# First normalisation of a two-block transformer kernel: tokens turned unscaled, scales applied to the outputs

## The chip, the cores and the metric

The kernel runs on one core of a Trainium2 chip. The metric is the device time of one execution in microseconds. A core has five engines with queues of their own: TensorE (PE; its weight loads are shown as PEld), VectorE (DVE), ScalarE (ACT), GpSimd (POOL) and SyncE (SP), which here issues the loads. They wait for each other through semaphores, which the kernel writes out by hand.

## What is computed

Two transformer blocks on 256 tokens of width 1024, all in float32. Only the opening of the first block is touched by the change:

```python
def rmsnorm(x, g):
    y = x * lax.rsqrt(jnp.mean(x * x, axis=-1, keepdims=True) + EPS)
    return y * g

hn = rmsnorm(h, attn_norm_g)
q, k, v, u, vg = jnp.split(hn @ w_in, [512, 1024, 1536, 2048], axis=-1)
sb_out = stick_breaking_attention(q, k, v)        # 8 heads of 64
sg_out = chunked_spatial_gating(u, vg, ...)       # u = gelu(u); vg = rmsnorm(gelu(vg))
h = h + concat(rmsnorm(sb_out), rmsnorm(sg_out)) @ w_out
```

Behind it come a mixture of 32 experts in 4 groups (top 1 group, top 2 experts), then a second block with differential attention, sparse attention, a cross-attention over a memory, and a layer that gathers rows of a large table (`in_uv`) for each token.

Since the norm multiplies each token (row of x) by one number s, and the gain multiplies each feature, (s x g) @ W = s ((x g) @ W): the number s can be applied before the product or to its outputs.

## The kernel before

**Operands.** Products with the input weights run in a rounded 32-bit type in three terms: a value is split into a high part (rounded) and a low part (what is left), and high*high, high*low and low*high are summed. For weights, ScalarE makes the high part (`high_quarters`, L192, 1024 columns at a time) and VectorE the low part (`low_quarters`, L199), each quarter of a 128x4096 piece. Pieces are `in0` (queries), `in1` (keys), `in4` (gate values, called g), `in3` (u), `in2` (v), `out0` and `out1`. There are two buffers for high parts, so `in4` waits until the query products are done with `in0`, and `in3` until the key products are done with `in1`.

**Tokens.** x (256 tokens, two tiles of 128) has to stand with its features on the partitions. `turn_pe` (L213) turns 16 blocks of 128x128 by TensorE into four PSUM banks, `turn_act` (L286) multiplies each of the eight chunks by the gain and rounds it (high part, XH), `turn_dve` (L293) makes its low part (XL).

**Order of the opening.** It is written by hand, an ordered list of steps for each engine (`a_pe`, `a_act`, `a_dve`), each of which raises the engine's semaphore by one. `mixers_sp` issues x, the identity, the small vectors, the first quarter of `in0`, its other three quarters, `in1`, `in4` and so on; `load_piece` waits until the piece two before has landed. When x is there, ScalarE (L300) and VectorE (L303) sum the squares of one token tile each, VectorE makes the mean (L297), GpSimd raises it to the power -1/2 (`rstd_pool`, L314), and ScalarE (L464) and VectorE (L306) each write one scaled tile into XZ. TensorE fills the time with products of no use (`spare`, 256 columns), turns XZ, and goes on, quarter by quarter as the parts arrive:

```python
turn_pe(pe, XZ, a_pe, "turn")
spare(pe, 6, 6)
turned_pair(pe, "in0", X2, a_dve, a_dve, "x", a_pe, 4)   # q0, q1
for m in (2, 3): turned(pe, "in0", ...)                  # q2, q3
for m in range(4):                                       # k0..k3, banks 2, 3, 2, 3
    if m >= 2: pe.wait_ge(*a_act.at(f"k{m - 2}"))
    turned(pe, "in1", ...)
```

The queries and keys come out turned (128 features x 256 tokens). ScalarE copies them from PSUM into `aq` (L472, times 0.125) and `ak` (L476). Then TensorE makes the scores (z0 to z2) and the units g (`in4`) and u (`in3`), in which the tokens are on the partitions. ScalarE rounds `in3`, takes Abs, Exp and Ln of the scores (L480, L485, L490), then GELU of g (L493), of u (L501), and later copies v. The u products wait for the GELU of g, since they write to the same banks.

**Behind it.** The units of the first block, the output projection, routing, and from about 130 us the experts, whose weights stream through eight slots; a slot's load is issued when TensorE has done with what it held (L185). The second block starts at about 583 us, and from 864 us on rows of `in_uv` are gathered by GpSimd (L2549) and multiplied (L2326).

## Time and profile before

| what | us |
|---|---|
| median of 3 runs | 1532.43 |
| lowest and highest | 1529.96, 1535.26 |
| profiled execution | 1534.07 |
| its span | 1532.0 |
| TensorE busy in it | 1252.2 (82%) |
| VectorE, ScalarE, GpSimd busy | 740.6, 469.5, 273.9 |
| bytes moved | 544.10 MB, mean 355 GB/s |

The span is the time from the first to the last instruction of the profiled execution; its own time lies 2.1 us above the span. In the rows below, L and a number is a line of the kernel, an arrow `<-` in an operation goes from what it reads to what it writes (out<-in), and `xN` counts instructions that were merged into one row. Matmuls overlap in the pipeline, so a duration of one is longer than the distance between two starts.

### The profile page before, as it was taken

How to read it: one execution, taken by the hardware profiler on the slowest of the kernel's cores; microseconds unless marked ns; L12 is line 12 of the kernel's file. 1: busy time of each engine (PE TensorE's matmuls, PEld its weight loads, DVE VectorE, ACT ScalarE, POOL GpSimd, SP SyncE). 2: the span in 40 equal slices, each digit the busy share in tenths (PEclk: the TensorE clock that was granted, in tenths of full speed). 3: DMA queues.
4: the chain of work that ended last, by engine and by line, in shares of the span. 5: the costliest groups of instructions: out<-in, count | busy, mean ns of one | idle time of the engine just before them, and what ended most of it. 6: DMA issues, size and time to landing. Idle time of an engine off the chain costs nothing.

```text
span 1532.0 us, 21054 instructions
## 1 busy us (share of the span) xinstructions
PE 1252.2 (82%) x8433; PEld 733.8 (48%) x8433; DVE 740.6 (48%) x1771; ACT 469.5 (31%) x1251; POOL 273.9 (18%) x287
## 2 busy tenths in 40 slices
PE   7999999999999987999999886888755645555465
PEld 7787565665555546977755453355311111111112
DVE  5544222212211115457722686676666676667454
ACT  5833011010100006456632244243323232323223
POOL 0000000000000001001000233434533333333331
PEclk9999999999999998999999999899977778777868
DMA  9548999999999998543471399999999999999996
GB/s 391 197 164 343 428 424 426 424 425 427 423 427 424 425 411 329 196 167 124 157 309 55 145 422 420 421 375 420 421 421 421 421 421 421 421 422 420 422 422 276
DMA packets 64583, 544.10 MB, mean 355 GB/s; under 512 B 6624, under 2 KB 7136, under 8 KB 12640
## 3 DMA queue, kind: packets, MB, share of 16 engines
q1 hardware_dynamic: 26160, 273.84, 43.6%
q0 software_dynamic: 38016, 268.45, 42.3%
q8 instruction: 69, 1.13, 0.3%
q10 hardware_dynamic: 304, 0.39, 0.1%
q14 instruction: 34, 0.28, 0.1%
HBM read 541.61 MB, written 1.05 MB: 354 GB/s over the span
## 4 chain that ended last, share of the span: by engine, by line
DMA 45%; PE 39%; DVE 5%; issue 4%; ACT 4%; POOL 2%; DVEq 0%; POOLq 0%; SPq 0%; ACTq 0%
PE PS L203 37%; DMA AR<-in_uv,CO 28%; DMA AR<-in_w_up 13%; DMA Wk<-in_w_up 2%; DMA EX<-in_w_up 2%; DVE AR L2326 2%; PE PS L213 2%; POOL AR L2549 1%; ACT HI L192 1%; ACT SM L2215 0%; ACT Wk L2221 0%; POOL AR L2525 0%; DMA CO<-in_const 0%; DVE XH L957 0%; ACT RW L2211 0%
## 5 line engine op out<-in xcount | busy, mean ns | idle before, releaser
L203 PE MATMUL PS<-AR,Wk 64*64 64x512 f32 (+4 forms) x2096 | 389.1, 716 | 186.3 <-ACT Wk L2221 179.6
L2326 DVE CUSTOM_DVE_ANT_0 AR<-AR,PS 128x1024 f32<-128x1024 f32 x192 | 233.9, 1221 | 171.2 <-DMA AR<-in_uv,CO 169.8
L203 PEld LDWEIGHTS PS<-AR,Wk 64*64 64x64 f32 (+3 forms) x2096 | 109.9, 157 | 417.8 <-ACT Wk L2221 282.5
L2549 POOL DMA_INDIRECT AR<-in_uv,CO x186 | 178.4, 959 | 295.1 <-PE PS L203 256.3
L203 PE MATMUL PS<-AR 128*64 128x256 f32 (+3 forms) x1656 | 192.3, 382 | 9.3 <-DMA AR<-in_w_up 8.7
L203 PEld LDWEIGHTS PS<-AR 128*64 128x64 f32 (+3 forms) x1656 | 119.7, 138 | 88.0 <-issue 19.3
L314 POOL TENSOR_TENSOR ST<-ST 128x2 f32<-128x2 f32 (+3 forms) x14 | 12.8, 915 | 779.4 <-DVE ST L1121 473.1
L2211 ACT ACTIVATE RW<-SM 128x2 f32<-128x2 f32 (+1 forms) x132 | 27.0, 205 | 395.3 <-DVE SM L2326 395.2
L199 DVE TENSOR_TENSOR LO<-AR,HI 128x1024 fp32r<-128x1024 f32 x76 | 89.5, 1225 | 54.6 <-ACT HI L192 54.6
L999 DVE TENSOR_TENSOR AR<-AR,PS 128x256 f32<-128x256 f32 x32 | 13.5, 422 | 195.1 <-ACT AR L856 195.1
L203 PE MATMUL PS<-Wk,AR 128*128 128x128 f32 (+2 forms) x816 | 97.5, 313 | 2.0 <-DMA Wk<-in_w_up 1.2
L203 PEld LDWEIGHTS PS<-Wk,AR 128*128 128x128 f32 (+1 forms) x816 | 83.7, 177 | 27.8 <-issue 12.5
L203 PE MATMUL PS<-XN,Wk 64*64 64x512 f32 (+1 forms) x368 | 66.3, 726 | 19.1 <-ACT Wk L2221 18.8
L1007 DVE SCALAR_TENSOR_TENSOR YL<-PS,Wk,YH 128x512 fp32r<-128x512 f32 x32 | 24.0, 751 | 112.3 <-ACT YH L860 112.3
L856 ACT ACTIVATE AR<-PS 128x256 f32<-128x256 f32 x32 | 12.3, 384 | 214.0 <-PE PS L203 214.0
L2221 ACT ACTIVATE Wk<-Wk,SM 128x64 f32<-128x64 f32 x256 | 75.5, 340 | 4.3
L192 ACT ACTIVATE HI<-AR 128x1024 fp32r<-128x1024 f32 x76 | 75.6, 1055 | 1.2 <-DMA AR<-in_w_in 1.2
L203 PE MATMUL PS<-HI,XH 128*128 128x512 f32 (+1 forms) x176 | 69.8, 397 | 4.2 <-ACT AR L1510 2.5
L203 PE MATMUL PS<-EX,Wk 64*64 64x512 f32 (+1 forms) x240 | 46.1, 781 | 26.2 <-ACT Wk L2221 26.2
L203 PE MATMUL PS<-HI,XL 128*128 128x512 f32 (+1 forms) x176 | 67.4, 383 | 0.0
L203 PE MATMUL PS<-LO,XH 128*128 128x512 f32 (+1 forms) x176 | 67.3, 382 | 0.0
L2215 ACT ACTIVATE SM<-RW 128x1 f32<-128x1 f32 x256 | 61.9, 287 | 12.8 <-ACT RW L2211 0.7
(308 smaller groups left out, 1803.8 us busy)
## 6 DMA issues: line engine op xcount, KB each, us to landing
AR<-in_w_up SPq DMA_DIRECT2D x24, 2048.0 KB, 14.7
AR<-in_w_down SPq DMA_DIRECT2D x24, 2048.0 KB, 14.7
AR<-in_w_gate SPq DMA_DIRECT2D x24, 2048.0 KB, 14.7
AR<-in_w_in SPq DMA_DIRECT2D x14, 2048.0 KB, 9.7
EX<-in_w_gate SPq DMA_DIRECT2D x4, 2048.0 KB, 15.3
Wk<-in_w_up SPq DMA_DIRECT2D x4, 2048.0 KB, 14.7
EX<-in_w_down SPq DMA_DIRECT2D x4, 2048.0 KB, 14.7
Wk<-in_w_gate SPq DMA_DIRECT2D x4, 2048.0 KB, 14.7
```

The source lines that it names most:

```text
L192: act.activation(hi[:, cs], w[:, cs], ACT.Copy).then_inc(*steps.up(f"{name}.{k}"))
L199: eng.tensor_tensor(lo[:, cs], w[:, cs], hi[:, cs].bitcast(F32), ALU.subtract).then_inc(*steps.up(f"{name}.{k}"))
L203: return pe.matmul(o, l, r, start=start, stop=stop, skip_group_check=True)
L213: return pe.transpose(o, i, ident[0:n, 0:n])
L314: pool.tensor_tensor(ST[:, a:b], ST[:, a:b], HALF[:, 0:b - a], ALU.pow).then_inc(*rms.up(site))
L999: dve.tensor_tensor(HM[:, b, :], SG[:, b, :], P(4 + b)[:, 256:512], ALU.mult).then_inc(*m_dve.up(f"h{ex}"))
L1007: dve.scalar_tensor_tensor(YL[:, b, :], P(6), SLOT_GATE[:, b:b + 1], YH[:, b, :].bitcast(F32), ALU.mult, ALU.subtract).then_inc(*m_dve.up( ...
L2211: act.activation(GEL[:, e:e + g1 - g0], DT[:, g0:g1], ACT.Gelu).then_inc(*a_own.up())
L2215: t = act.activation(DT[:, g:g + 1], BGf[:, g:g + 1], ACT.Copy, scale=GEL[:, e + g - g0:e + g - g0 + 1])
L2221: act.activation(DG[:, g % 8, :], ID64, ACT.Copy, scale=DT[:, g:g + 1]).then_inc(diags, 1)
L2326: t = dve.tensor_tensor_reduce(r, r, P(6 if g < 128 else 2, 2), 1.0, 0.0, ALU.mult, ALU.add, DT[:, g:g + 1])
L2549: pool.indirect_dma_start(RING[k], None, uv, bass.IndirectOffsetOnAxis(ap=IDX[:, g:g + 1], axis=0)).then_inc(g_in[k], 16)
```

## The change

- TensorE turns x itself (`H`) as soon as it and the identity have landed. XZ is no longer written with scaled tokens.
- ScalarE and VectorE begin with the turned chunks x0 and x1, then take the first quarter of `in0`, then the other chunks. The squares are summed behind the quarters of `in0`.
- GpSimd's power and the mean stay as they are, later. Of the two resulting columns VectorE makes two diagonal matrices; TensorE multiplies them by a matrix of ones, behind the queries (step `wide`), so that each partition holds the scales of all 256 tokens; VectorE copies this to `WIDE_X`.
- VectorE, no longer ScalarE, takes queries and keys out of PSUM, multiplied by `WIDE_X`, interleaved with the low parts of `in4`.
- For g, u and v, which have tokens on the partitions, ScalarE applies the scale as the operand of its GELU or copy.
- The first 16 spare products of 256 columns become 32 of 128 columns with zeros, which wait for the zeros alone.

Step lists (`a_pe`, `a_act`, `a_dve`) follow; they are left out of the diff.

```diff
@@ -348,6 +348,9 @@
         T1 = w2(3072)
         VG = w2(1024, "p (t n) -> p t n", t=2)
         blocks = [(0, 0), (0, 1), (1, 1)]
+        WIDE_X = MX[:, 0, 0:256]
+        DIAG_X = MX[:, 1, 0:256].rearrange("p (t n) -> p t n", t=2)
+        ONES_X = MX[:, 0, 256:384]
 
         def mixers_sp(sp):
             sp.dma_start(H, x.rearrange("(t p) d -> p t d", p=128)).then_inc(ld_x, 16)
@@ -373,22 +376,25 @@
 
         def mixers_pe(pe):
             pe.wait_ge(wm_set, 1)
-            spare(pe, 6, 8)
-            pe.wait_ge(*a_dve.at("mean"))
-            spare(pe, 6, 8)
+            for _ in range(32):
+                mm(pe, P(6)[:, 0:128], WMt[:, 128:256], WMt[:, 128:256], True, True)
             pe.wait_ge(ld_id, 16)
-            pe.wait_ge(*a_act.at("xs0"))
-            pe.wait_ge(*a_dve.at("xs1"))
-            turn_pe(pe, XZ, a_pe, "turn")
+            pe.wait_ge(ld_x, 16)
+            turn_pe(pe, H, a_pe, "turn")
+            pe.wait_ge(wm_set, 2)
             spare(pe, 6, 6)
             turned_pair(pe, "in0", X2, a_dve, a_dve, "x", a_pe, 4)
             for m in (2, 3):
                 turned(pe, "in0", X2, P(m % 2)[:, 0:256], m).then_inc(*a_pe.up(f"q{m}"))
+            for tt in range(2):
+                pe.wait_ge(*a_dve.at(f"diag{tt}"))
+                t = mm(pe, P(6)[:, tt * 128:tt * 128 + 128], ONES_X, DIAG_X[:, tt, :], True, True)
+            t.then_inc(*a_pe.up("wide"))
             for m in range(4):
                 if m >= 2:
-                    pe.wait_ge(*a_act.at(f"k{m - 2}"))
+                    pe.wait_ge(*a_dve.at(f"k{m - 2}"))
                 turned(pe, "in1", X2, P(2 + m % 2)[:, 0:256], m, *((a_dve,) if m == 0 else ())).then_inc(*a_pe.up(f"k{m}"))
-            pe.wait_ge(*a_act.at("k3"))
+            pe.wait_ge(*a_dve.at("k3"))
             for b, (kt, qt) in enumerate(blocks):
                 for h in range(8):
                     r = slice(64 * (h % 2), 64 * (h % 2) + 64)
@@ -402,6 +408,7 @@
                         pe.wait_ge(*a_act.at(f"{before}{tt}"))
                     tokens(pe, name, X2, P(6 + tt), tt, *((a_dve,) if tt == 0 else ())).then_inc(*a_pe.up(f"{tag}{tt}"))
 
+            pe.wait_ge(*a_dve.at("wide"))
             unit("in4", "g", None)
             unit("in3", "u", "g")
             pe.wait_ge(ld_co, 16)
@@ -458,22 +465,17 @@
                     out_part_pe(pe, j, tt, range(4)).then_inc(*a_pe.up(f"r{j}{tt}"))
 
         def mixers_act(act):
+            act.wait_ge(ld_sm, 16)
+            turn_act(act, X2, sm["g_attn"], a_act, "x", a_pe, "turn", range(2))
+            high_quarters(act, "in0", a_act, range(1), (ld_in0, 16))
+            turn_act(act, X2, sm["g_attn"], a_act, "x", a_pe, "turn", range(2, 8))
+            high_quarters(act, "in0", a_act, range(1, 4))
             act.wait_ge(ld_x, 16)
-            square_sum(act, H[:, 0, :], XS[:, 0, :], ST[:, 0:1]).then_inc(*a_act.up("sq"))
-            act.wait_ge(*rms.at("x"))
-            act.activation(XZ[:, 0, :], H[:, 0, :], ACT.Copy, scale=ST[:, 0:1]).then_inc(*a_act.up("xs0"))
-            act.wait_ge(ld_sm, 16)
-            high_quarters(act, "in0", a_act, range(1), (ld_in0, 16))
-            turn_act(act, X2, sm["g_attn"], a_act, "x", a_pe, "turn")
-            high_quarters(act, "in0", a_act, range(1, 4))
+            square_sum(act, H[:, 0, :], XZ[:, 0, :], ST[:, 0:1]).then_inc(*a_act.up("sq"))
             high_quarters(act, "in1", a_act)
-            for m in range(4):
-                act.wait_ge(*a_pe.at(f"q{m}"))
-                act.activation(aq[:, m, :], P((4, 5, 0, 1)[m])[:, 0:256], ACT.Copy, scale=0.125).then_inc(*a_act.up(f"q{m}"))
+            act.wait_ge(*a_pe.at("q3"))
             high_quarters(act, "in4", a_act)
-            for m in range(4):
-                act.wait_ge(*a_pe.at(f"k{m}"))
-                act.activation(ak[:, m, :], P(2 + m % 2)[:, 0:256], ACT.Copy, scale=1.0).then_inc(*a_act.up(f"k{m}"))
+            act.wait_ge(*a_pe.at("k3"))
             high_quarters(act, "in3", a_act)
             for b in range(3):
                 act.wait_ge(*a_pe.at(f"z{b}"))
@@ -488,9 +490,10 @@
             for b in range(3):
                 l = T1[:, b * 1024:(b + 1) * 1024]
                 act.activation(l, l, ACT.Ln, bias=1.0).then_inc(*a_act.up(f"ln{b}"))
+            act.wait_ge(*rms.at("x"))
             for tt in range(2):
                 act.wait_ge(*a_pe.at(f"g{tt}"))
-                act.activation(VG[:, tt, :], P(6 + tt), ACT.Gelu_apprx_tanh).then_inc(*a_act.up(f"g{tt}"))
+                act.activation(VG[:, tt, :], P(6 + tt), ACT.Gelu_apprx_tanh, scale=ST[:, tt:tt + 1]).then_inc(*a_act.up(f"g{tt}"))
             act.wait_ge(*a_act.at("g1"))
             for tt in range(2):
                 t = square_sum(act, VG[:, tt, :], MX[:, tt, 512:1024], ST[:, 4 + tt:5 + tt])
@@ -498,7 +501,7 @@
             high_quarters(act, "in2", a_act)
             for tt in range(2):
                 act.wait_ge(*a_pe.at(f"u{tt}"))
-                act.activation(U1[:, tt, :], P(6 + tt), ACT.Gelu_apprx_tanh).then_inc(*a_act.up(f"u{tt}"))
+                act.activation(U1[:, tt, :], P(6 + tt), ACT.Gelu_apprx_tanh, scale=ST[:, tt:tt + 1]).then_inc(*a_act.up(f"u{tt}"))
             high_quarters(act, "out0", a_act)
             for b in range(3):
                 l = T1[:, b * 1024:(b + 1) * 1024]
@@ -514,7 +517,7 @@
             t.then_inc(*a_act.up("sqg"))
             for tt in range(2):
                 act.wait_ge(*a_pe.at(f"v{tt}"))
-                act.activation(AV[:, tt, :], P(6 + tt), ACT.Copy).then_inc(*a_act.up(f"v{tt}"))
+                act.activation(AV[:, tt, :], P(6 + tt), ACT.Copy, scale=ST[:, tt:tt + 1]).then_inc(*a_act.up(f"v{tt}"))
             turn_act(act, X2, sm["g_mix"], a_act, "m", a_pe, "turn2", range(4, 8))
             high_quarters(act, "out1", a_act)
             act.wait_ge(*a_pe.at("pv"))
@@ -527,22 +530,40 @@
             zeros = AR[:, 6 * 4096:6 * 4096 + 128]
             dve.memset(zeros, 0.0).then_inc(*own.up())
             dve.wait_ge(*own.at())
-            dve.tensor_copy(WMt[:, 128:256], zeros)
+            dve.tensor_copy(WMt[:, 128:256], zeros).then_inc(wm_set, 1)
             dve.wait_ge(ld_id, 16)
             dve.tensor_copy(WMt[:, 0:128], ident).then_inc(wm_set, 1)
+            dve.wait_ge(ld_sm, 16)
+            turn_dve(dve, X2, sm["g_attn"], a_act, a_dve, "x", range(2))
+            low_quarters(dve, "in0", a_act, a_dve, range(1))
+            turn_dve(dve, X2, sm["g_attn"], a_act, a_dve, "x", range(2, 8))
+            low_quarters(dve, "in0", a_act, a_dve, range(1, 4))
+            dve.memset(ONES_X, 1.0).then_inc(*a_dve.up("ones"))
             dve.wait_ge(ld_x, 16)
-            square_sum_dve(dve, H[:, 1, :], XS[:, 1, :], ST[:, 1:2]).then_inc(*a_dve.up("ss"))
+            square_sum_dve(dve, H[:, 1, :], XZ[:, 1, :], ST[:, 1:2]).then_inc(*a_dve.up("ss"))
             dve.wait_ge(*a_act.at("sq"))
             dve.wait_ge(*a_dve.at("ss"))
             mean(dve, ST[:, 0:2], D).then_inc(*a_dve.up("mean"))
             dve.wait_ge(*rms.at("x"))
-            scaled(dve, XZ[:, 1, :], H[:, 1, :], ST[:, 1:2]).then_inc(*a_dve.up("xs1"))
-            dve.wait_ge(ld_sm, 16)
-            low_quarters(dve, "in0", a_act, a_dve, range(1))
-            turn_dve(dve, X2, sm["g_attn"], a_act, a_dve, "x")
-            low_quarters(dve, "in0", a_act, a_dve, range(1, 4))
-            for name in ("in1", "in4", "in3"):
-                low_quarters(dve, name, a_act, a_dve)
+            for tt in range(2):
+                scaled(dve, DIAG_X[:, tt, :], ident, ST[:, tt:tt + 1]).then_inc(*a_dve.up(f"diag{tt}"))
+            low_quarters(dve, "in1", a_act, a_dve)
+            dve.wait_ge(*a_pe.at("wide"))
+            dve.tensor_copy(WIDE_X, P(6)[:, 0:256]).then_inc(*a_dve.up("wide"))
+            dve.wait_ge(*a_dve.at("wide"))
+
+            def evac(dst, tag, banks, ms, scale=1.0):
+                for m in ms:
+                    dve.wait_ge(*a_pe.at(f"{tag}{m}"))
+                    dve.scalar_tensor_tensor(dst[:, m, :], P(banks[m])[:, 0:256], scale, WIDE_X, ALU.mult, ALU.mult).then_inc(
+                        *a_dve.up(f"{tag}{m}"))
+
+            evac(aq, "q", (4, 5, 0, 1), range(4), 0.125)
+            low_quarters(dve, "in4", a_act, a_dve, range(2))
+            evac(ak, "k", (2, 3, 2, 3), (0,))
+            low_quarters(dve, "in4", a_act, a_dve, range(2, 4))
+            evac(ak, "k", (2, 3, 2, 3), (1, 2, 3))
+            low_quarters(dve, "in3", a_act, a_dve)
             dve.wait_ge(ld_co, 16)
             for b, (kt, qt) in enumerate(blocks):
                 s = SPL[:, b * 1024:(b + 1) * 1024]
```

## Rows read from the trace of the kernel before

**Rows 1.** The page, chain that ended last: shares of the span by engine
```profile
DMA 45%; PE 39%; DVE 5%; issue 4%; ACT 4%; POOL 2%; DVEq 0%; POOLq 0%; SPq 0%; ACTq 0%
```

**Rows 2.** Chain of waits in order of time: start us, us, what
```profile
1.25 4.60 DMA CO<-in_const
...
7.61 0.71 POOL ST L314
...
16.11 21.86 PE PS L203 x180
...
38.00 0.38 ACT Wk L476
...
54.12 30.72 PE PS L203 x128
...
317.63 14.69 DMA AR<-in_w_up
...
1114.70 34.62 DMA AR<-in_uv,CO
```

**Rows 3.** DMA issues of the first 60 us: count, KB each, us to landing
```profile
AR<-in_w_in SPq DMA_DIRECT2D x1, 1536.0 KB, 10.3
```

**Rows 4.** Timeline of the first 17 us: start us, us, engine, work, [idle before <-releaser]
```profile
1.02 0.23 DVE L530 CAST WM<-AR 128x128 fp32r<-128x128 f32 x1
...
2.69 0.45 SPq L357 DMA_DIRECT2D AR<-in_w_in  x1
...
6.15 3.78 PE L203 MATMUL PS<-WM 128*128 128x256 f32 x16 [6.15 <-DVE WM L532]
...
9.40 1.04 ACT L192 ACTIVATE HI<-AR 128x1024 fp32r<-128x1024 f32 x1
...
9.73 2.65 PE L213 MATMUL PS<-CO,AR 128*128 128x128 f32 x16
10.54 1.23 DVE L199 TENSOR_TENSOR LO<-AR,HI 128x1024 fp32r<-128x1024 f32 x1 [1.44 <-ACT HI L192]
10.82 3.03 ACT L286 ACTIVATE XH<-PS,SM 128x256 fp32r<-128x256 f32 x8 [0.38 <-PE PS L213]
11.70 3.23 DVE L293 SCALAR_TENSOR_TENSOR XL<-PS,SM,XH 128x256 fp32r<-128x256 f32 x8
...
13.69 3.00 ACT L192 ACTIVATE HI<-AR 128x1024 fp32r<-128x1024 f32 x3
...
14.84 3.49 DVE L199 TENSOR_TENSOR LO<-AR,HI 128x1024 fp32r<-128x1024 f32 x3
...
16.11 0.39 PE L203 MATMUL PS<-XH,HI 128*128 128x256 f32 x1 [1.58 <-DVE LO L199]
```

**Rows 5.** Timeline of the first expert, TensorE's loads of weights
```profile
138.86 0.31 PEld L203 LDWEIGHTS PS<-WM,PG 128*128 128x128 f32 x2
...
139.09 0.19 PEld L203 LDWEIGHTS PS<-PG,XGH 128*128 128x128 f32 x1
```

**Rows 6.** TensorE by line and form: count, busy us, mean ns, idle before
```profile
L203 PE MATMUL PS<-Wk,AR 128*128 128x128 f32 x512 | 62.8, 283 | 0.8 <-ACT Wk L1840 0.8
```

**Rows 7.** Timeline of ScalarE, and of VectorE in the first expert
```profile
17.86 3.91 ACT L192 ACTIVATE HI<-AR 128x1024 fp32r<-128x1024 f32 x4 [1.17 <-DMA AR<-in_w_in]
...
38.28 3.89 ACT L192 ACTIVATE HI<-AR 128x1024 fp32r<-128x1024 f32 x4
...
53.48 1.09 ACT L493 ACTIVATE AR<-PS 128x512 f32<-128x512 f32 x2
...
138.16 0.42 DVE L999 TENSOR_TENSOR AR<-AR,PS 128x256 f32<-128x256 f32 x1 [5.09 <-ACT AR L856]
```

**Rows 8.** Waits by engine and line, 0 to 60 us: total, times, longest
```profile
PE PS L203 <- ACT AR L493: 1.6, 1, 1.6
```

**Rows 9.** Stretches: busy us of PE, PEld, DVE, ACT, POOL; PEclk, DMA share, GB/s
```profile
584.00:596.00 12.00, 5.44 (x24) 5.20 (x25) 9.32 (x15) 9.37 (x16) 1.01 (x1) 0.53 0.97 407
596.00:620.00 24.00, 23.71 (x189) 23.50 (x188) 13.05 (x20) 12.91 (x21) 5.68 (x2) 0.95 0.55 216
```

More of the change, by code:

```diff
@@ L325, in program @@
         gated, broken = [f"m{c}" for c in range(4, 8)], fours("m")
-        a_pe = Steps(sem("a_pe"), [*split_steps("turn"), *fours("q"), *fours("k"), "z0", "z1", "z2", *twos("g"), *twos("u"),
+        a_pe = Steps(sem("a_pe"), [*split_steps("turn"), *fours("q"), "wide", *fours("k"), "z0", "z1", "z2", *twos("g"), *twos("u"),
                                    "sum0", "sum1", "sum2", "space", *twos("v"), "turn2.2", "turn2.3", "pv", "turn2.0", "turn2.1",
                                    "r00", "r01", "r10", "r11"])
-        a_act = Steps(sem("a_act"), ["sq", "xs0", "in0.0", *eights("x"), "in0.1", "in0.2", "in0.3", *split_steps("in1"), *fours("q"),
-                                     *split_steps("in4"), *fours("k"), *split_steps("in3"), "abs", "exp", "ln0", "ln1", "ln2",
+        a_act = Steps(sem("a_act"), ["x0", "x1", "in0.0", *eights("x")[2:], "in0.1", "in0.2", "in0.3", "sq", *split_steps("in1"),
+                                     *split_steps("in4"), *split_steps("in3"), "abs", "exp", "ln0", "ln1", "ln2",
                                      *twos("g"), "sqv", *split_steps("in2"), *twos("u"), *split_steps("out0"), "e0", "e1", "e2", "sqg",
                                      *twos("v"), *gated, *split_steps("out1"), "sqb", *broken])
-        a_dve = Steps(sem("a_dve"), ["ss", "mean", "xs1", "in0.0", *eights("x"), "in0.1", "in0.2", "in0.3", *split_steps("in1"),
-                                     *split_steps("in4"),
+        a_dve = Steps(sem("a_dve"), ["x0", "x1", "in0.0", *eights("x")[2:], "in0.1", "in0.2", "in0.3", "ones", "ss", "mean", "diag0", "diag1",
+                                     *split_steps("in1"), "wide", *fours("q"), "in4.0", "in4.1", "k0", "in4.2", "in4.3", "k1", "k2", "k3",
                                      *split_steps("in3"), "sp0", "sp0m", "sp1", "sp2", "sp2m", "meanv", "vg", *split_steps("in2"),
```

## The prediction

> **What bounds the kernel now.** I read the page first, then the chain of waits over the first 130 us, then the timeline of each engine over the first 60 us, and last what bounds the rest. The shares of the chain [rows 1] say what the whole is made of: DMA 45% and PE 39%. The change touches the first 54 us of 1532 directly, so the question is what is late there, and whether a microsecond won there reaches the end.
>
> The chain [rows 2] shows three links of the opening: POOL's power of the norm at 7.61, then PE's unbroken 21.86 us of query and key products (180 of them, 0.121 us each) from 16.11, then ScalarE from 38.00 until PE takes over at 54.12. From there PE leads until the expert weights do (317.63, a wait of 14.69 us for a piece of w_up), and at the end the gathered rows (34.62 us in one wait). Everything behind 54 us is started by steps of PE or by what they release; what comes earlier there should come earlier at the end, less whatever a transfer takes back.
>
> The opening in detail: x and identity have landed by 5.85 [rows 2]. Then squares, mean, power and two scaled copies run before PE may turn anything: the turns start at 9.73 [rows 4]. But the turned tokens are only one of two things that PE wants. The other is in0. Its last three quarters are issued at 2.69 [rows 4] and land 10.3 later [rows 3], at 12.99. ScalarE rounds them from 13.69, VectorE subtracts from 14.84, and PE, idle for 1.58, goes on at 16.11 [rows 4]. So of the whole norm chain only the 0.70 between 12.99 and 13.69 is not covered by the load of in0. That is what I expect to be worth having, and it is the point at which I part from the obvious count (the turns could start 3.8 earlier).
>
> **Part by part.**
>
> Norm out of the way. Removed ahead of the turns: squares, mean, power, two scaled copies. ScalarE now has x0 and x1, then the first quarter of in0 (landed by 9.40, where it starts now [rows 4]), then x2 to x7. The first quarter ends at 10.4; six turned chunks at 3.03/8 = 0.38 [rows 4] bring it to 12.7. The next quarter then waits for the landing at 12.99 instead of starting at 13.69. VectorE follows ScalarE by 10.54 - 9.40 = 1.14 in this pattern. Its first low quarter runs 10.54 to 11.77, six chunks at 3.23/8 = 0.40 end at 14.2, and the second quarter of in0 can be subtracted from 12.99 + 1.14 = 14.13. Two limits that nearly coincide; PE resumes at 15.41 instead of 16.11. **Gain 0.70.**
>
> Warm-up products. 16 of 256 columns behind the identity become 32 of 128 columns from 1.27, as soon as the zeros are written [rows 4]. Before, 16 took 3.58 (6.15 to 9.73 [rows 4]), 0.22 each. Products with 128 columns of this rounded type stand in the expert stage only: two of them, whose loads take 0.31 for two with 0.19 for one, come 0.12 apart at the full clock [rows 5]. They are as slow as those with twice the columns. So the bounds are 0.11 each at the low clock (half of 0.22) and 0.25 (twice 0.12). I take 0.22, as the 0.12 row is the nearest in kind: until the clock rises 24 or so, then the rest at 0.12, together some 6, ending at 7.3. The first turns then wait 1.5 behind them, yet x0 and x1 are ready by 8.7, before the first quarter of in0 has landed. **Cost nothing**, because the load hides it; without that cover it would be 1.5. The Trainium skill (TensorE: Matmul & The Clock Gate, Wait — 56ns, not 53.3ns?) gives 107 ns for 128 columns cold and 56 ns warm; by it the 32 would be over at 4.7, before x has landed, and the row (0.12 warm) speaks against it for this type.
>
> Spreading the scales. Two products of ones with a diagonal, 128x128 in plain f32, go between queries and keys on PE's queue, where nothing hides them. Such products cost between 62.8/512 = 0.12 [rows 6] and their full 0.28 with 0.2 for the change of type. Bounds for the pair 0.25 to 0.77; I take 0.5. They wait for the diagonals, ready at 20.4 (VectorE: in0's lows to 17.6, ones and squares 1.4, mean 0.2, POOL 0.71 [rows 2] and handing over, two small scalings), well before queries end at 25.6. **Cost 0.5.**
>
> Copies of queries and keys move from ScalarE to VectorE. A pass over 128x256 from PSUM with a second operand is 0.42 [rows 7] against 0.38. VectorE's queue: in1's lows end at 25.0 (20.4 and four at 1.16); it waits there for the wide products at 26.1; the copy and four query passes end at 28.2; two quarters of in4 at 30.5; k0 at 31.0. PE needs the bank of k0 for k2 at 26.1 + 5.8 = 31.9. k1 is copied at 33.7 and wanted at 34.8. **Cost nothing**, slack 0.9 and 1.1. Queued behind VectorE's wait for the wide products is everything up to in3's lows; PE itself waits for it only at k2, k3 and the scores.
>
> ScalarE no longer copies k3 before it rounds in3. That copy starts at 38.00 [rows 2] and in3's quarters at 38.28 [rows 7], behind it. Now they start as PE ends the keys. From there to the first GELU at 53.48 ScalarE never waits [rows 7], and PE sat idle 1.6 waiting for it [rows 8]. So this 0.28 is on the path, and the scores, 0.04 later behind VectorE's pass, are covered by in3's four quarters (3.89). **Gain 0.28.**
>
> Scales on GELU and on v: a per-partition operand in place of a constant. ScalarE's turned chunk with such an operand is 0.38, the k3 copy without one 0.38. Nothing. ScalarE's squares now fall between in0 and the landing of in1 (it waits until 17.86 anyway [rows 7]). No DMA is added or moved; SP's waits for queries and keys fall 0.2 to 0.7 earlier.
>
> Sum: -0.70 + 0.5 - 0.28 = **-0.5 us**. The profiled execution took 1534.07 (span 1532.0), so it would be 1533.6; it lies 1.6 above the median of the runs, 1532.43, and against that median the forecast is **1531.9**. About 0.3% (4.6 us) is what a measurement can tell from no change; the three runs alone lie 5.3 apart. So: no measurable change.
>
> **Rivals.**
>
> PE's clock falls in the opening. Until now PE pauses once, for 1.58 [rows 4]. After the change it has done its warm-up and turns by about 10, waits for the first low quarter until 11.8, works 1.4, waits until 15.4. Later in this kernel 12 us with PE busy for 5.4 had a granted clock of 0.53, and the 24 behind it, full work, 0.95 [rows 9]. At the low one of the two levels, 1.2 GHz, a product costs 0.22 instead of 0.121, and PE's run is on the path. 24 us at 0.95 is 2.4 at the low level, 1.2 lost: net +0.7. If it stayed low for all of the 84 queries left and more, the loss is 0.1 a product: 50 products cost 5, and from there on the kernel is slower measurably; all 84 cost 8.4, net +7.9, 1540.3. For it: the opening has less PE work per microsecond than before. From 7.3 to 15.4 it has about 4 us of work in 8, hardly more than those 5.4 in 12. Against: here the pauses are of 1.8 and 2.2, and it comes to them at the full clock from unbroken work. The Trainium skill (TensorE: Matmul & The Clock Gate, HAM oscillation — how this bites in real kernels) warns of just this, that waits for loads between bursts put the array back to half rate; by that rule the gain is gone.
>
> Warm-up too long. At 0.25 each the 32 end at 9.3; turns, x0 and x1 come at 11.0, in0's first quarter at 12.0, VectorE's chunks at 15.7, PE resumes at 17.0: 0.9 late, net +1.1, 1533.5.
>
> VectorE becomes the bound. If its six passes before k2 took 0.84 each, k2 would stall by 1.6, net +1.1. Against: 0.42 in the trace and slack 0.9.
>
> The full norm chain was what mattered. Then PE resumes up to 3.8 earlier, net -3.6, 1528.8. Against it is the landing of in0 at 12.99; even so it would not be measurable.
>
> **How the numbers follow.** Forecast (a gain of up to 1 us) 0.50, clock falls briefly 0.27, clock stays low 0.04, warm-up too long 0.10, VectorE 0.05, full chain 0.04. Only one of them is beyond 4.6 us. The rest of both tails is the scatter of 5.3 between equal runs. Faster 0.05, same 0.89, slower 0.06. Range: from the full chain's 1528.8 less a little scatter, 1528.0, to the warm-up's 1533.5 with 2.5 of scatter and a little more for a clock low for 20 or 30 products, 1536.5.
>
> **What would show it.** PE's first turn near 7.3 (4.7: products at 0.11; 9.3: at 0.25). in0's second quarter rounded at 13.0 behind a landing, not behind ScalarE's own work. PE back at 15.4. Two wide products costing about 0.5 between queries and keys. in3's quarters at 37.8 on ScalarE, GELU at 53.0, PE's u products at 53.6 (54.12 before). Granted clock 1.00 from 12 to 54. Wrong if PE resumes before 15 (the landing is not the bound), if query products run at 0.2 apart, or if the 0.5 is not seen at the first expert.

## The result and the profile after

The changed kernel takes 1536.63 us (median of 20 runs) against 1532.47 for the kernel before (20 runs): a ratio of 1.0027, interval 1.002 to 1.0034. It is 4.1 us slower. The forecast was 1531.9, no measurable change, with a range up to 1536.5. One of the 20 runs of the changed kernel took 2582 us and is not in the ratio.

| landmark in the profiled execution | before | after | later by |
|---|---|---|---|
| PE resumes with the second quarter of in0 | 16.11 [rows 2] | 17.24 | 1.13 |
| in3's quarters on ScalarE, behind the keys | 38.28 [rows 7] | 41.06 | 2.78 |
| PE starts the u products | 54.12 [rows 2] | 57.01 | 2.89 |
| execution (span) | 1534.07 (1532.0) | 1539.85 (1537.8) | 5.8 |

This execution lies 3.2 above the median of its kernel. The page of it:

```profile
span 1537.8 us, 21101 instructions
...
PE 1267.4 (82%) x8453; PEld 742.3 (48%) x8453; DVE 742.9 (48%) x1782; ACT 466.4 (30%) x1242; POOL 274.8 (18%) x287
...
PE 47%; DMA 37%; issue 5%; ACT 4%; DVE 4%; POOL 1%; DVEq 0%; POOLq 0%; ACTq 0%; SPq 0%
```

DMA's share of the chain was 45% and is 37%, PE's 39% and is 47%. That is no effect of the change: a second profile of the same changed kernel has 43% and 41%, and one with ScalarE's table load moved ("Table load early" below) 52% and 30%. ScalarE's opening (start us, us, engine, line, work, [idle before]):

```profile
9.36 1.28 ACT L286 ACT_TABLE_LOAD   x1 [9.36 <-PE PS L213]
10.66 0.84 ACT L286 ACTIVATE XH<-PS,SM 128x256 fp32r<-128x256 f32 x2
11.38 1.06 ACT L192 ACTIVATE HI<-AR 128x1024 fp32r<-128x1024 f32 x1
12.33 2.29 ACT L286 ACTIVATE XH<-PS,SM 128x256 fp32r<-128x256 f32 x6
14.47 3.00 ACT L192 ACTIVATE HI<-AR 128x1024 fp32r<-128x1024 f32 x3
```

The first row was not in the count: a load of ScalarE's function table, 1.28 us, now begins only when the first turns are done. TensorE's side of the same stretch:

```profile
1.31 7.09 PE L203 MATMUL PS<-WM 128*128 128x128 f32 x32 [1.31 <-DVE WM L533]
8.20 3.46 PE L213 MATMUL PS<-CO,Hs 128*128 128x128 f32 x16
11.41 0.96 PE L203 MATMUL PS<-WM 128*128 128x256 f32 x6
...
17.24 0.39 PE L203 MATMUL PS<-XH,HI 128*128 128x256 f32 x1 [1.79 <-DVE LO L199]
```

The 32 warm-up products last 7.09 (0.22 each, to the last), so the turns (the 16 blocks of x that TensorE turns) start at 8.20 and not at 5.9, and all 16 of them run at the low pace as well, 0.21 each, where eight turns later in this kernel take 0.87. The granted clock of the profile reads 1.00 in this stretch all the same, as it does in the opening of the kernel before; that TensorE is at the lower of its two levels here is read from the pace alone. The chain of waits, start us, us, what:

```profile
17.24 23.80 PE PS L203 x184
...
41.06 3.90 ACT HI L192 x4
...
57.01 30.74 PE PS L203 x128
...
133.57 6.45 PE PS L203 x57
```

From 17.24 to the end of the keys PE takes 23.80 instead of 21.86 [rows 2]. Two stretches of it (busy us of PE, PEld, DVE, ACT, POOL; then PEclk, DMA share, GB/s):

```profile
16.00:20.00 4.00, 2.76 (x16) 2.77 (x17) 4.00 (x6) 4.00 (x6) 0.00 (x0) 0.77 0.99 426
20.00:26.00 6.00, 6.00 (x46) 6.00 (x45) 5.07 (x9) 2.29 (x3) 0.75 (x2) 0.87 1.02 426
```

The granted clock was 0.77 and 0.87 there, so 0.23 x 4 + 0.13 x 6 = 1.7 us of full clock were lost by these figures; it was 1.00 in the kernel before. A profile without the fall, below, puts the loss at 1.49.

### The profile page after: what moved, and what is told of

The parts are those of the page before. It is cut to its first block, busy times and chain, and to the rows that moved or that the text cites. A ratio compares the mean times of both kernels' runs of the same rounds, so it can differ in the third digit from the quotient of the medians.

```text
span 1537.8 us, 21101 instructions
## 1 busy us (share of the span) xinstructions
PE 1267.4 (82%) x8453; PEld 742.3 (48%) x8453; DVE 742.9 (48%) x1782; ACT 466.4 (30%) x1242; POOL 274.8 (18%) x287
## 3 DMA queue, kind: packets, MB, share of 16 engines
q8 instruction: 69, 1.13, 0.3%
HBM read 541.61 MB, written 1.05 MB: 353 GB/s over the span
## 4 chain that ended last, share of the span: by engine, by line
PE 47%; DMA 37%; issue 5%; ACT 4%; DVE 4%; POOL 1%; DVEq 0%; POOLq 0%; ACTq 0%; SPq 0%
PE PS L203 46%; DMA AR<-in_uv,CO 25%; DMA AR<-in_w_up 9%; DMA EX<-in_w_up 2%; PE PS L213 2%; DVE AR L2347 1%; DMA Wk<-in_w_up 1%; ACT HI L192 1%; DMA XN<-in_uv,CO 1%; POOL AR L2570 0%; ACT Wk L2242 0%; ACT SM L2236 0%; POOL AR L2546 0%; ACT Wk L1861 0%; DVE XH L978 0%
## 5 line engine op out<-in xcount | busy, mean ns | idle before, releaser
L203 PE MATMUL PS<-AR,Wk 64*64 64x512 f32 (+4 forms) x2096 | 396.2, 731 | 178.6 <-ACT Wk L2242 161.8
L203 PEld LDWEIGHTS PS<-AR 128*64 128x64 f32 (+3 forms) x1656 | 119.6, 138 | 88.8 <-issue 19.1
L203 PE MATMUL PS<-Wk,AR 128*128 128x128 f32 (+2 forms) x816 | 100.8, 316 | 4.2 <-issue 2.3
L203 PE MATMUL PS<-XN,Wk 64*64 64x512 f32 (+1 forms) x368 | 65.0, 709 | 16.4 <-ACT Wk L2242 15.5
```

The lines of the kernel that those rows point to most:

```text
L203: return pe.matmul(o, l, r, start=start, stop=stop, skip_group_check=True)
```

## The experiments

Each result is a ratio to runs of the kernel before on the same chip. The kernels are told as edits of the changed kernel where nothing else is said.

### Table load early

```diff
+            act.wait_ge(*rms.at("half"))
+            act.activation(ST[:, 62:63], HALF[:, 0:1], ACT.Copy)
             act.wait_ge(ld_sm, 16)
```

> The changed kernel with one tiny ScalarE copy (one column) put ahead of its first waits, so that the 1.28 us load of ScalarE's function table, which in the changed kernel begins at 9.36 behind the first turns, falls into the empty time before x lands. Theory (the table load is on the path of the opening): ScalarE's first turned chunk starts at 9.36 instead of 10.66, the second quarter of in0 is rounded from 13.2 instead of 14.47, PE resumes at 16.0 instead of 17.24, and its u products start 1.2 earlier than 57.01 if the clock falls as before (about 55.8), 2.7 earlier if it doesn't. Total 1.2 to 2.7 below the changed kernel's 1536.6, about 1535. Rival (the landing of in0 at 13.0 and the turns at 8.4 hold it anyway): PE resumes at 17 or later, no difference. Second rival for the clock: it falls again at 18.2 for 3.4 us, as PE's work before it is the same.

Ratio 1.0015 (1.0006 to 1.0024), 1534.95 us. ScalarE's timeline, then the chain:

```profile
0.72 1.28 ACT L469 ACT_TABLE_LOAD   x1 [0.72 <-PEq L2722]
...
9.38 0.84 ACT L286 ACTIVATE XH<-PS,SM 128x256 fp32r<-128x256 f32 x2 [7.16 <-PE PS L213]
...
13.20 3.00 ACT L192 ACTIVATE HI<-AR 128x1024 fp32r<-128x1024 f32 x3
```

```profile
15.96 22.30 PE PS L203 x184
...
54.23 30.73 PE PS L203 x128
```

The load falls into the empty time at 0.72 and everything behind it is 1.28 earlier, as expected. The clock did not fall at all here, so u starts 2.8 earlier, 0.1 behind the kernel before. The opening was put right, and the total was still 2.3 above the kernel before (0.0015 x 1532.9). A pause of 1.25 stands in the turns of the second block, which the next experiments are about.

### Twelve warm-up products

```diff
-            for _ in range(32):
+            for _ in range(12):
```

> The changed kernel with 12 instead of 32 warm-up products, which also brings TensorE's count of instructions back to that of the kernel before. Theory: the 32 products at 0.22 us each (7.09 us) hold up the turns from 5.9 to 8.4, and the table load starts when the first turns are done. With 12 they end at 4.0, turns start at 5.9, the table load at 6.9, x0 at 8.1, first quarter of in0 at 9.4, PE resumes at 15.4, which is 1.8 earlier. If the clock is up by then, u starts 1.8 earlier than 57.01 (55.2), 3.3 earlier if it doesn't fall (53.7). Rival (warm-up is needed for the clock): the granted clock is half for more of the queries than the 3.4 us of the changed kernel, each 3.4 us costing 1.5, and u starts no earlier than 56. On the rest: a pause of 1.29 us in the middle of the turns of the second block (597.87 to 599.16 in the changed kernel, none in the kernel before), which the profile puts down to nothing but issue, is a fetch of TensorE's code; with the old count of instructions it should go, and the second block's first products come 1.0 earlier against the first expert. If it stays, it isn't the count.

Ratio 0.9995 (0.9986 to 1.0004), 1532.75 us: the kernel before's time. ScalarE's timeline:

```profile
7.23 1.28 ACT L286 ACT_TABLE_LOAD   x1 [7.23 <-PE PS L213]
...
12.83 2.95 ACT L192 ACTIVATE HI<-AR 128x1024 fp32r<-128x1024 f32 x3 [0.34 <-DMA AR<-in_w_in]
```

The table load starts at 7.23 and is hidden (the first turns are ready earlier, as they wait for 12 products only), and the second quarter of in0 now starts behind its landing (the idle time is ended by the DMA). This is the bound that the forecast named; PE resumes at 15.20. But the chain shows that this gain of 0.9 was lost again before u:

```profile
15.20 10.80 PE PS L203 x88
...
32.22 6.03 PE PS L203 x48
...
54.22 5.98 PE PS L203 x25
```

Between the 88 products from 15.20 and k2 at 32.22 VectorE is in the chain. Its rows, and GpSimd's:

```profile
27.82 4.01 DVE L199 TENSOR_TENSOR LO<-AR,HI 128x1024 fp32r<-128x1024 f32 x2
31.75 0.41 DVE L558 SCALAR_TENSOR_TENSOR Wk<-PS,Wk 128x256 f32<-128x256 f32 x1
```

```profile
27.20 2.41 POOL L626 TENSOR_TENSOR Wk<-Wk,CO 128x1024 f32<-128x1024 f32 x1 [7.50 <-DMA Wk<-in_w_sp]
```

Two low quarters took 4.01 where they take 2.35 elsewhere, k0 was taken out of PSUM at 31.75 and k2 had waited 0.49 for it. They met GpSimd's multiplication of the spatial weights, which ended at 29.61: the trace has the first of the two at 2.88 (27.82 to 30.70) and the second at 1.21. The second block's turns had no pause.

### Without pauses on TensorE

```diff
+            act.wait_ge(*rms.at("half"))
+            act.activation(ST[:, 62:63], HALF[:, 0:1], ACT.Copy)
...
-            for _ in range(32):
-                mm(pe, P(6)[:, 0:128], WMt[:, 128:256], WMt[:, 128:256], True, True)
+            for _ in range(20):
+                mm(pe, P(6)[:, 0:256].rearrange("p (a n) -> p a n", a=2), WMt[:, 128:256],
+                   bc(WMt[:, 128:256].unsqueeze(1), [128, 2, 128]), True, True)
...
-            spare(pe, 6, 6)
+            spare(pe, 6, 16)
```

and 13 spare products more ahead of the second quarter of in0. The 20 products have 256 columns, all zeros.

> The changed kernel with the early table load, 20 warm-up products of 256 columns of zeros in place of 32 of 128, 16 spare products in place of 6 behind the turns, and 13 more between the first and the second quarter of in0, so that TensorE has hardly a pause. Theory (three things hold it: table load 1.3, late turns, clock 1.5): the turns start at 5.9, PE resumes at 15.4, no fall of the clock at 18, keys end at 37.7, u starts at 53.7 (54.12 before, 57.01 changed). Total 3.3 below the changed kernel by the opening, about 1533, or 1532 if the pause in the second block goes as well: the same as before, not faster. Rival (the first product of the change, unscaled turning, can't reach below the landing of in0): the same 15.4; if PE resumes under 15 the landing is not the bound. Rival on the clock: it falls in spite of the fill, u at 55.2.

Ratio 1.0011 (1.0000 to 1.0023), 1534.49 us. The opening came as expected: PE resumes at 15.01, the landing still the bound, the turns faster (16 in 2.54 instead of 3.46), u at 53.29, which is 0.8 earlier than in the kernel before. The total is nevertheless 1.7 above it. The loss is in the second block, whose spare products before the turns read:

```profile
589.13 1.62 PE L203 MATMUL PS<-WM 128*128 128x256 f32 x6 [6.10 <-issue]
594.34 1.01 PE L203 MATMUL PS<-WM 128*128 128x256 f32 x3 [3.59 <-issue]
```

A pause of 3.59 that the profile puts down to nothing but issue. The label alone says little, since the idle time of about 6 before the nine spare products is called issue in some executions (6.10 here) and VectorE's in others (5.71 in the kernel before). But between the sixth and the seventh spare product the code has no wait. This kernel has 11 more products ahead of the second block than the changed one (8464 against 8453 on the page), and the pause stands 10 products earlier in the program: 3 spare ones and 7 turned blocks. It sits at a place in the code, not at a moment in time.

### The kernel before with 20 more products

```diff
             pe.wait_ge(wm_set, 1)
+            for _ in range(20):
+                mm(pe, P(6)[:, 0:128], WMt[:, 128:256], WMt[:, 128:256], True, True)
+            pe.wait_ge(wm_set, 2)
             spare(pe, 6, 8)
...
-            dve.tensor_copy(WMt[:, 128:256], zeros)
+            dve.tensor_copy(WMt[:, 128:256], zeros).then_inc(wm_set, 1)
```

> The kernel before with 20 products of 128 columns of zeros put ahead of its own warm-up, done before the identity lands, so that nothing in its opening moves, but TensorE's code has the changed kernel's count of instructions. Theory (1.0 of the 4.2 is a fetch of code that has moved into the turns of the second block): opening as before (PE resumes at 16.1, u at 54.1, first expert at 130.6), pause of about 1.3 in the second block's turns, its first products 1.0 later, total 1.0 above the kernel before. Rival (the 1.0 comes from the phase of the clock in the second block, shifted by the late opening, or from scatter): no pause, total the same as before within 0.5.

> The kernel before with 20 early products once more, as the interval of its first runs (0.06% to 0.24%) leaves open whether the shifted code costs 0.9 or 3.7. Theory: 1.0 to 1.5 above the kernel before, pause of about 1.1 in the second block's turns again at the eighth block. Rival (the first result was scatter): within 0.5 of the kernel before.

Ratios 1.0015 (1.0006 to 1.0024) and, on another chip, 1.0010 (1.0000 to 1.0019): 2.3 and 1.5 us, with an opening that is the old one (u at 54.19 and 54.25). Some 1.0 was expected; the intervals, 0.9 to 3.7 and 0.0 to 2.9 us, allow it. The second run's turns in the second block:

```profile
592.48 1.95 PE L213 MATMUL PS<-CO,AR 128*128 128x128 f32 x8 [0.49 <-ACT AR L1464]
595.48 1.97 PE L213 MATMUL PS<-CO,AR 128*128 128x128 f32 x8 [1.05 <-issue]
```

Twenty products that do nothing, in time that was empty, cost 1.5 to 2.3 us 590 us later. The changed kernel has the same pause at the same place (here behind the seventh block, above behind the eighth); the code has no wait between the 16 turns:

```profile
596.13 1.73 PE L213 MATMUL PS<-CO,AR 128*128 128x128 f32 x7 [0.92 <-ACT AR L1482]
599.16 2.08 PE L213 MATMUL PS<-CO,AR 128*128 128x128 f32 x9 [1.29 <-issue]
```

### The changed kernel again

> The changed kernel, unchanged, for a second profile. Open is whether the fall of the granted clock at 18.2 for 3.4 us is part of the change or of that one execution (its 1539.85 lay 3.2 above the median of its runs). Theory: it is of the execution; in this profile the queries may run unbroken, from 17.2 to 27.4, the keys end at 39.5 and u starts at 55.5, 1.4 later than in the kernel before. Rival: the clock falls again, u at 57.0. In both the pause of some 1.3 in the second block's turns is there, as the count of instructions is the same, and the first eight turned blocks stand on the same side of it. Total 1536.6 within 0.7.

Ratio 1.0040 (1.0025 to 1.0056), 1537.84 us, from 6 runs: 6.1 us above the kernel before, where the first measurement gave 4.1 and 1536.6 within 0.7 was expected. The two intervals, 3.8 to 8.6 and 3.1 to 5.2 us, overlap. Its chain:

```profile
17.24 22.31 PE PS L203 x184
...
55.52 30.74 PE PS L203 x128
```

PE resumes at 17.24 again, the clock does not fall, and 184 products take 22.31: u starts 1.40 late instead of 2.89. The fall at 18 is of the execution, not of the kernel. The difference of 22.31 to the 21.86 for 180 [rows 2] is the price of spreading the scales, 0.45 (184 and 180 count instructions; the two products of the step are four). The pause is there again:

```profile
594.99 1.73 PE L213 MATMUL PS<-CO,AR 128*128 128x128 f32 x7 [0.84 <-ACT AR L1482]
597.85 2.08 PE L213 MATMUL PS<-CO,AR 128*128 128x128 f32 x9 [1.13 <-issue]
```

### A long warm-up in few products

```diff
-            for _ in range(32):
-                mm(pe, P(6)[:, 0:128], WMt[:, 128:256], WMt[:, 128:256], True, True)
+            blank(pe, 16)
...
-            spare(pe, 6, 6)
+            spare(pe, 6, 2)
```

Each `blank` product has 512 columns of zeros.

> The changed kernel with its long warm-up kept in time but not in count: 16 products of 512 columns of zeros (about 0.43 each, 6.8 in all) for 32 of 128, and 2 spare products for 6 behind the turns, which brings TensorE's instructions to the count of the kernel before. Table load late, turns late as in the changed kernel. Theory (the late opening and the code fetch are two separate costs): PE resumes at 17.0 to 17.3, u at 55.4 to 57.0, no pause in the second block's turns, total 1.0 to 1.5 below the changed kernel's, about 1535.3. Rival (the count costs nothing by itself; the total follows the opening alone): 1536.6.

Ratio 1.0004 (0.9993 to 1.0015), 1532.48 us. It did not separate what it was made to separate:

```profile
1.31 5.33 PE L203 MATMUL PS<-WM 128*128 128x512 f32 x16 [1.31 <-DVE WM L537]
...
15.29 0.38 PE L203 MATMUL PS<-XH,HI 128*128 128x256 f32 x1 [0.77 <-DVE LO L199]
```

The 16 took 5.33, 0.33 each: eight start 0.43 apart, the rest 0.23, so the clock went up on the way. So they ended at 6.6, and PE resumed at 15.29; the opening was early. The 32 of 128 columns had stayed at 0.22 for 7.09.

### GpSimd's multiplication moved away

```diff
             rstd_pool(pool, a_dve.at("mean"), "x", 0, 2)
+            rstd_pool(pool, a_dve.at("meanv"), "vg", 4, 6)
             pool.wait_ge(ld_ws, 16)
             pool.wait_ge(ld_co, 16)
             pool.tensor_tensor(WS, WS, ...)
-            rstd_pool(pool, a_dve.at("meanv"), "vg", 4, 6)
```

with 12 warm-up products as above.

> The kernel with 12 warm-up products, and GpSimd's multiplication of the spatial weights (2.4 to 3.1 us at 25.95) moved behind its next power of a norm at about 56. In the kernel with 12, PE resumed at 15.2, 0.9 earlier than in the kernel before, yet u started at 54.22, no earlier: VectorE's two low quarters of in4 took 4.01 instead of 2.35 at 27.82, while GpSimd worked, k0 was taken out at 31.75 and k2 waited for it. Theory (VectorE and GpSimd slow each other on these operands): with GpSimd quiet the two take 2.35, k0 leaves at 30.1, no gap before k2, keys end at 37.5, u at 53.5. Rival (something else held VectorE; the gap stays): two quarters again at 4.0, u at 54.2. Total 1532.0 against 1532.75.

Ratio 0.9994 (0.9984 to 1.0004), 1532.21 us. VectorE, and the chain:

```profile
28.09 2.35 DVE L199 TENSOR_TENSOR LO<-AR,HI 128x1024 fp32r<-128x1024 f32 x2
30.36 0.42 DVE L558 SCALAR_TENSOR_TENSOR Wk<-PS,Wk 128x256 f32<-128x256 f32 x1
```

```profile
15.47 22.31 PE PS L203 x184
...
53.76 30.73 PE PS L203 x128
```

With GpSimd quiet there the two quarters take 2.35 and nothing stands between 15.47 and the end of the keys. u is 0.46 earlier than with 12 products alone, although PE resumed 0.27 later.

### Everything found, at the old count

Early table load, 10 warm-up products of 512 columns, 4 behind the turns in place of 6 spare ones, 4 ahead of the second quarter of in0, GpSimd's work moved.

> All that was found, at the old count of TensorE's instructions: early table load, 10 warm-up products of 512 columns of zeros, 4 such behind the turns for 6 spare ones, 4 more between the first and second quarter of in0, GpSimd's multiplication later. Theory: turns at 5.9, PE resumes at 15.0, no clock fall, keys end at 37.3, u at 53.3 (54.12 before), the second block as in the kernel before, all 0.8 earlier; total about 1531.7 to 1532.0, faster than the kernel before by 0.05%, not to be told from it. Rival (the second block's clock or its gathers take it back): 1532.9.

Ratio 0.9999 (0.9989 to 1.0008), 1532.09 us:

```profile
15.19 22.30 PE PS L203 x184
...
53.46 30.73 PE PS L203 x128
```

u starts 0.66 earlier than in the kernel before, and no pause is in the second block. The time is that of the kernel before.

### Late opening, old code positions

```diff
-            spare(pe, 6, 26)
+            blank(pe, 6, 13)
...
-            spare(pe, 3, 14)
+            blank(pe, 3, 7)
```

Each `blank` product has 512 columns of zeros. The opening keeps its 20 products more; from the routing on, the code stands where it stood in the kernel before.

> The changed kernel, its opening left alone (32 warm-up products, late turns, late table load), with 20 products taken out behind it: the 26 and 14 spare products of 256 columns in the routing become 13 and 7 of 512 columns of zeros, so that from there on TensorE's code stands at the places of the kernel before. This is the separation that the run with 16 long products failed to give, since its clock rose at 4.3 and its opening got early. Theory (the late opening and the shifted code are two costs that add): PE resumes at 17.2, u at 55.5 (57.0 in an execution whose clock falls), no pause in the second block's turns, total 1.45 below the changed kernel's 1536.6: 1535.2, that is 2.7 above the kernel before. Rival (the shifted code costs nothing outside one profile): 1536.6. Second rival (the count is all of it): 1532.9.

Ratio 1.0007 (0.9998 to 1.0016), 1534.05 us. Chain, and the second block's turns:

```profile
17.25 23.79 PE PS L203 x184
...
57.01 30.73 PE PS L203 x128
```

```profile
595.87 3.30 PE L218 MATMUL PS<-CO,AR 128*128 128x128 f32 x16 [0.92 <-ACT AR L1487]
```

The opening is that of the changed kernel, the fall of the clock included, and the 16 turns are in one row again. The total is 1.1 above the kernel before (-0.3 to 2.5). The 2.7 expected is just outside that; the second rival, that the count is all of it (0.4), is inside. So this run shows that the pause goes with the positions; the loss falls by 3.0 with it, known to about 2. It does not show what the late opening costs by itself.

> The same with the early table load as well. Theory: PE resumes at 16.0, u at 54.2, no pause in the second block's turns; as late as the kernel before and with its code positions, so the same total, 1532.5 to 1533.0. Rival (something else in the changed kernel costs a microsecond that neither the opening nor the count explains): 1534 or more.

Ratio 0.9996 (0.9987 to 1.0005), 1532.91 us; PE resumes at 15.96, u at 55.72, since the clock fell in this execution; no pause. Level with the kernel before.

### What they say together

Times over the kernel before, in us (ratio less 1, times 1532.5). "Shifted" means that the second block's code for TensorE stands that many products later than in the kernel before:

| opening | code shifted by 20 products | old positions |
|---|---|---|
| changed, table load late | +4.1, +6.1 | +1.1 |
| changed, table load early | +2.3 | -0.6 |
| early (PE resumes at 15.0 to 15.5) | +1.7 (shifted by 31) | -0.8, +0.6, -0.9, -0.2 |
| of the kernel before | +2.3, +1.5 | 0 |

The shift costs 3.0 (5.0 by the second measurement), 2.9, 2.0, and 2.3 or 1.5: some 2.5. Each entry has an interval of about 1.4 either way, so each of these differences is known to about 2 us and their mean to about one. The late table load costs 1.8 and 1.7 by this table, where the traces show 1.28. No entry at the old positions can be told from 0, so the totals do not show that the late opening costs anything by itself; that rests on the traces.

The shift is more than the 1.05 to 1.29 of its pause. Two figures of the second block show where more of it lies. One is the distance from the issue of the memory to that of the next piece of w_in2, which spans the turns and the first products. The other is the time at the low clock from 584 to 620 (twice what the granted clocks of 584:596 and 596:620 lack to 1):

| execution | distance, us | at low clock, us |
|---|---|---|
| before, old positions | 20.0 | 13.7 |
| 12 products; long; GpSimd moved; all found; late; late with table | 19.7, 18.8, 18.8, 18.8, 18.8, 19.0 | 10.6, 10.3, 10.3, 10.3, 10.3, 10.3 |
| shifted: changed, changed again, table early | 20.9, 22.2, 21.3 | 13.7, 17.0, 13.7 |
| shifted: kernel before, twice | 19.6, 21.1 | 10.3, 13.9 |
| shifted by 31: without pauses | 21.9 | 13.7 |

Mean 19.1 at the old positions, 21.0 shifted by 20. The pause lies in the work that brings the clock back up, and in five of six shifted executions, against one of seven others, the clock also stayed low longer. These are single executions, one profile of each run, and the link is a count of cases, not an experiment.

## Why the prediction was wrong

**The landing of in0 as the bound** was right, and worth what was said: with turns in time PE resumes at 15.0 to 15.5 (15.41 forecast), behind a wait that the DMA ends. The changed kernel does not get there.

**"The first turns then wait 1.5 behind them ... Cost nothing"**, for the warm-up products, failed in part. The pace was right (0.22) but the clock was to rise on the way and did not, so they ended at 8.40 and not 7.3 (by its own terms, 24 x 0.22 + 8 x 0.12, it should have said 7.5). The Trainium skill (TensorE: Matmul & The Clock Gate, Wait — 56ns, not 53.3ns?) would have them at 107 ns; the trace, for this type, does not agree. The rival with 0.25 a product named the mechanism; the low clock throughout was its form. That it put PE's return at 17.0, near the measured 17.24, is luck: it had no table load, and its products were to end at 9.3. By itself the late end of the warm-up was still nearly covered: with the early table load PE resumes at 15.96, 0.55 behind the forecast.

**ScalarE's list of instructions was not complete.** The rule that every instruction of a moved step counts was broken where it was hidden: the table load stood at the head of ScalarE in the kernel before, in time that nobody used, and had no row among those read. With ScalarE's first work moved behind a wait for TensorE it went there too: 1.28, on the path. This is the first step that failed: "gain 0.70" became 1.13 lost, by 1.28 of table load and 0.55 of late turns, 1.83 in all.

**"Wide" products 0.5:** 0.45, by four instructions and not two; the product behind them starts 0.20 after the one before instead of 0.12, so the change of type cost 0.08 there, and the 0.2 taken for the upper bound was generous. **Copies moved to VectorE, nothing:** right in the changed kernel, and the slack of 0.9 was real but thin: in the run with 12 products VectorE's wait for GpSimd took it. That is the rival of VectorE as the bound, brought on by GpSimd and not by the passes themselves (0.42 each as said). **in3's quarters without the k3 copy, 0.28 gained:** PE ends the keys at 41.03 and the quarters start at 41.06, against 38.28 behind 37.98; 0.27. **Scales on GELU, nothing:** wrong by 0.1 for each. A row of ScalarE's groups (mean ns of one: 599 in the kernel before):

```profile
L504 ACT ACTIVATE Wk<-PS,ST 128x512 f32<-128x512 f32 x2 | 1.4, 689 | 4.8 <-PE PS L203 4.8
```

**The opening, then:** -0.5 forecast; 1.40 measured without a fall of the clock: 1.13 + 0.45 - 0.28 + 0.1. With the fall it is 1.49 more.

**The rival of the clock** came true in the first profile at about its price (1.2 said), in the second it did not. Of the five profiled executions that start the turns near 8.2 three have a granted clock of 0.63 to 0.80 from 16 to 20; those with early turns have 1.00. In the three that fell, the six spare products behind the turns took 0.96 to 1.00, so the clock was up by then; in the two that did not, they took 1.53 and 1.63, most of them still at the low pace. Why the clock rises sooner in one execution of a kernel than in another is open. The one with 16 long products has 0.68 from 12 to 16, after TensorE had waited 2.94; the low time fell mostly on twelve products of the first quarter, behind which TensorE had to wait 0.77 for the second quarter anyway, so it cost nothing. The Trainium skill (TensorE: Matmul & The Clock Gate, HAM oscillation — how this bites in real kernels) warned of a fall behind waits for loads, and the traces agree in kind: the three falls come behind waits of 0.6 to 1.8 in the opening (1.79 in the changed kernel).

**That what comes at 54 us comes at the end** was right as far as it went. From the u products to the issue of the memory in the second block all thirteen profiled executions, the kernel before's among them, take 534.3 to 535.5. But the sum had no term for code that moves, and this is the second step that failed: +20 products, counted as hidden work, are also +20 products of code, put at nothing, and they cost some 2.5 (1.5 to 3.0 in all pairs but the one with 5.0) of the 4.1. No row of the kernel before shows it, as its own turns are in one piece there. It was the missing rival, and the upper end of the range, 1536.5, was made up without it; the measured 1536.63 lies 0.1 above that end.

Is the pause a fetch of code? Shown is that it stands at one count of instructions. In each of the six executions that have it, 4077 weight loads of TensorE lie ahead of it, whether the code is shifted by 20 products or by 31. The profile also lists packets of kind "instruction"; the page of the changed kernel (packets, MB, share):

```profile
q8 instruction: 69, 1.13, 0.3%
```

The kernel before has 69 as well, of 16 KB each. In the six executions TensorE goes on 2.2 to 2.4 after the start of one such packet (in the changed kernel the packet starts at 596.8 and TensorE at 599.16; in the run without pauses 592.15 and 594.34). In the seven executions at the old positions the packet of the same number starts 3.7 to 5.6 before TensorE comes to that count, among the query products, and there is no pause. This fits a fetch that comes too late, and explains why the same count costs nothing at the old positions. It is not proven: that this queue brings TensorE's code is inferred, no run moved the packet alone, and what sets its start is open. So is what the shift costs beyond these 1.9 of distance, if anything.

## What to carry to other kernels

When the first work of an engine is moved behind a wait, look for what stood at its head without being written: here a table load of 1.28 us went with it; a one-column activation on a constant, ahead of the waits for loads and for TensorE, kept it in the empty time. Products "for nothing" are not free of side effects: count what they add to TensorE's instructions, and compare a kernel at equal counts before a microsecond is explained by its schedule. A gain of less than 1 us in the opening (0.66 here, well shown in the trace) is below what 1532 us of run time let one see.

## What the runs showed of the hardware

- 32 products of 128 columns of zeros, back to back from 1.31, ran at 0.22 us each for 7.09 us, where such products take 0.12 later [rows 5], in all five profiled executions that have them. The 16 turned blocks behind them took 3.46 to 3.64 in four of the five and 2.93 in one, where the pace doubled after ten. Behind 20 products of 256 columns from the same moment, with almost no pause, the turns took 2.54. At the low level a product of 128 columns takes as long (0.22) as one of 256 [rows 4].
- VectorE's subtraction of two tensors and GpSimd's product of two did not run at once. A subtraction that started at 27.82 beside a product that ended at 29.61 took 2.88 and not 1.21; in the kernel before one from 27.85 beside a product that ended at 28.40 took 1.63. Both ended 1.1 after GpSimd. In the changed kernel GpSimd's product started at 25.95, beside a subtraction that ended at 26.80, and took 3.10 and not 2.40.
- In the kernel before one wait (for x) stands ahead of ScalarE's first activation, and the table load did not wait for it (0.72, the activation 5.69). In the changed kernel there are two, and the load came behind both, at 9.36.
- TensorE paused at one count of its instructions (4077 weight loads), for 1.05 to 1.29 in five executions and 3.59 in one; it went on 2.2 to 2.4 behind the start of a packet of kind "instruction".
